# A fused two-layer transformer kernel: the delta rule of half the tokens moved between the second half's input products, the rest beside sparse attention and output products

## What is computed

```python
h = rmsnorm(x, g_pre) * (1.0 + scale) + shift
qkv_a, z_a, b_a, a_a, q_b, ckv, z_b, iq, ik, iw = split(h @ w_in)
# gated delta rule, 4 heads of 128, on silu(causal_conv(qkv_a, conv_w))
q, k = l2norm(q) * 128**-0.5, l2norm(k)
lmat = strict_lower((beta * k) @ k.T * decay)
tmat = inverse(eye + lmat)            # per chunk
v_new = tmat @ (beta * v) - (tmat @ (beta * k * exp(gc))) @ S
o = (q * exp(gc)) @ S + (q @ k.T * decay) @ v_new
S = S * exp(gc_last) + kg.T @ v_new
o_a = rmsnorm(o, g_gdn) * silu(z_a)
# sparse attention: per query the top keys by an index score, softmax with a
# distance bias over the compressed keys ckv, then w_uv
o_b = (softmax(q_b @ ckv.T * 128**-0.5 + bias, selected) @ ckv @ w_uv) * silu(z_b)
x = x + gate * rmsnorm(concat(o_a, o_b) @ w_out, g_post)
```

## Time and profile before

| what | us |
|---|---|
| median of three runs | 2534.99 |
| span of the profiled execution | 2543.5 |
| PE busy in it | 2028.3 (80%) |
| DVE busy | 1644.6 (65%) |
| ACT busy | 801.4 (32%) |
| POOL busy | 662.6 (26%) |
| `second_half` | from 2035.1 to about 2211.6 |
| `sparse` | to about 2263.9 |
| `delta` | to the end |

### The profile page before, as it was taken

One profiled execution on the slowest core, in us unless ns is written; L12 is line 12 of the kernel. 1 busy time (PEld: TensorE's weight loads), 2 busy tenths in 40 slices (PEclk: granted clock), 3 DMA queues, 4 the chain that ended last, 5 costly groups with the idle time before them and its releaser, 6 DMA issues. The chain is left out here.

```text
span 2543.5 us, 31869 instructions
## 1 busy us (share of the span) xinstructions
PE 2028.3 (80%) x11958; PEld 1321.8 (52%) x11958; DVE 1644.6 (65%) x3770; ACT 801.4 (32%) x1791; POOL 662.6 (26%) x657
## 2 busy tenths in 40 slices
PE   4999968696876798788698778859787688756886
PEld 3888858562331365454365456415333266636664
DVE  5668876589786766554768667587964417944442
ACT  2112220233423424532434543353222231231221
POOL 2222100233444333433333243343344200000000
PEclk9999989898987899999799888878999869977889
DMA  8998752399999999999899798999999833110000
GB/s 333 368 358 304 268 197 67 148 419 408 381 421 421 416 418 410 420 396 386 346 394 360 277 367 344 378 404 368 419 420 419 331 102 100 66 74 1 9 9 17
DMA packets 124682, 746.74 MB, mean 294 GB/s; under 512 B 13536, under 2 KB 16480, under 8 KB 56304
## 3 DMA queue, kind: packets, MB, share of 16 engines
q0 software_dynamic: 93792, 610.66, 60.2%
q1 hardware_dynamic: 30736, 134.05, 13.7%
HBM read 741.25 MB, written 3.41 MB: 293 GB/s over the span
## 5 line engine op out<-in xcount | busy, mean ns | idle before, releaser
L1766 POOL DMA_INDIRECT got<-in_peer_uv,idx x512 | 587.4, 1147 | 950.8 <-PE ps L1736 804.5
L1736 PE MATMUL ps<-got,diag 64*64 64x512 f32 x3936 | 607.8, 705 | 284.5 <-ACT diag L1823 266.3
L1860 DVE CUSTOM_DVE_ANT_0 got<-got,xk 128x1024 f32<-128x1024 f32 x512 | 616.1, 1221 | 253.5 <-DMA got<-in_peer_uv,idx 247.0
L1736 PEld LDWEIGHTS ps<-got,diag 64*64 64x64 f32 x3936 | 119.3, 146 | 564.0 <-ACT diag L1823 471.1
L1818 ACT ACTIVATE gelu<-eye,hid 128x64 f32<-128x64 f32 x492 | 169.9, 345 | 664.4 <-DVE hid L1860 662.9
L1325 PE MATMUL ps<-xT,ring 128*128 128x256 f32 x928 | 224.5, 393 | 6.6 <-DVE qkv L1414 6.6
L1325 PEld LDWEIGHTS ps<-xT,ring 128*128 128x128 f32 x928 | 173.7, 194 | 86.4 <-issue 48.0
L1027 PE MATMUL ps<-xT,ring 128*128 128x256 f32 x768 | 188.9, 395 | 1.7 <-ACT xT L1140 1.7
L1823 ACT ACTIVATE diag<-gelu,gate 128x64 f32<-128x64 f32 x492 | 171.1, 348 | 51.4 <-PE ps L1736 6.1
L1027 PEld LDWEIGHTS ps<-xT,ring 128*128 128x128 f32 x768 | 143.3, 194 | 77.1 <-issue 47.0
L192 POOL DMA_DIRECT2D vring<-in_vslabs x136 | 72.4, 533 | 275.3 <-DVE in_b_psums L304 139.5
(11 more groups left out here) (564 smaller groups left out, 2599.8 us busy)
## 6 DMA issues: line engine op xcount, KB each, us to landing
ring<-in_small SPq DMA_DIRECT2D x158, 512.0 KB, 7.9
vring<-in_vslabs POOLq DMA_DIRECT2D x136, 512.0 KB, 6.2
ring<-in_slabs SPq DMA_DIRECT2D x18, 2048.0 KB, 10.5
got<-in_peer_uv,idx POOLq DMA_INDIRECT x512, 13.2
h<-in_x SPq DMA_DIRECT2D x2, 2048.0 KB, 11.3
w_out<-in_slabs SPq DMA_DIRECT2D x2, 2048.0 KB, 11.3
out<-h SPq DMA_DIRECT2D x4, 512.0 KB, 2.6
bias_rows<-brow POOLq DMA_DIRECT2D x1, 1280.0 KB, 5.7
```

The costliest lines, as they stand in the source:

```text
L1736: mm = nc.tensor.matmul(ps[to:to + HALF, i, :], diag[own, d % NDIAG, :], got[own, n % GRING, 1, 512 * g:512 * g + 512], start=(k == 0), st ...
L1766: nc.gpsimd.indirect_dma_start(out=got[:, n % GRING].rearrange("p a d -> p (a d)"), out_offset=None, in_=table, in_offset=bass.IndirectOff ...
L1860: nc.vector.tensor_tensor_reduce(row_in, row_in, xk[:, w % 2, :], 1.0, 0.0, ALU.mult, ALU.add, hid[:, w % 2, k:k + 1]).then_inc(dotted, 1)
```

## The change

The delta rule is cut into functions of one step (`delta_tiles`), as are sparse attention (`sparse_tiles`), the output products (`mixed_tiles`) and the decay gates (`decay_gates`), and two blocks take the place of three stages.

- `second_half` carries, besides what it had, the decay gates of half a (steps 1 to 6) and of half b (45 to 49), the delta rule of tile 0 (steps 6 to 33) and tile 1 (33 to 60), one delta step per step, and sparse attention of tile 0 (48 to 62). PSUM: the delta rule has banks 0 to 2; the input products have 3 to 5 in turn (a product waits for the third before it); the rest shares 6 and 7.
- For half b the convolution's two copies and first tap are ScalarE's, with two buffers; VectorE keeps three taps. A product's bank is free once ScalarE has copied it.
- The Silu of half a's qkv and z_a move to the end of ScalarE's program in `peers`; half a's z_b and half b's qkv have theirs at step 57. Table sets are loaded by hand behind each.
- `gp_spread` and its product move from ahead of the steps to steps 20 to 23, the bias rows to every second step from 14.
- `recycle` is called between the two blocks.
- `second_rest` loads the output weights and walks one hand-made list of 43 steps: tiles 2 and 3 of the delta rule (tile 3 three steps behind), sparse attention of tiles 1 to 3, and output products of tiles 0 to 3. The output rows are squared by ScalarE out of PSUM and multiplied by the gain by VectorE out of PSUM, without a copy.
- In the head, row sums come ahead of the transposes, v is transposed at NORM, and the three token transposes wait each for their own operand.

```diff
@@ second_side
+        bank_of = lambda n: ps[:, 3 + (n - 4) % 3 if p and n >= 4 else 4 + n % 4, :]
+        back = 3 if p else 4
...
+                        elif p and second_jobs[before][0] == "qkv":
+                            pe.wait_ge(raw_out, second_jobs[before][1] + 1)
...
+                    elif p and kind == "qkv":
+                        mine = raw[:, i % 2, :]
+                        if i >= 2:
+                            act.wait_ge(dve_out, len(on_dve) + i - 1)
+                        step(nc.scalar.activation(mine[:, 0:3], halo[:, i, :], ACT.Copy))
+                        act.wait_ge(job_done, n - 3)
+                        nc.scalar.activation(mine[:, 3:3 + 2 * P], bank[:, 0:2 * P], ACT.Copy).then_inc(raw_out, 1)
+                        act.wait_ge(raw_out, i + 1)
+                        nc.scalar.activation(tap[:, i % 2, :], mine[:, 0:2 * P], ACT.Copy, scale=cw[:, 0, i:i + 1]).then_inc(tap_out, 1)
...
+                        mine, one = raw[:, i % 2, :], tap[:, i % 2, :]
+                        dve.wait_ge(tap_out, i + 1)
+                        for j in (1, 2):
+                            step(ve.scalar_tensor_tensor(one, mine[:, j:j + 2 * P], cw[:, j, i:i + 1], one, ALU.mult, ALU.add))
@@ peers, ScalarE
                     move(NW - 1)
+                    act.wait_ge(sides[2]["dve_out"], len(dve_jobs))
+                    for name in ("qkv", "z_a"):
+                        nc.scalar.activation(half_a[name], half_a[name], ACT.Silu)
@@ second_block
-                second_half(halves, whole, gp_row, gain_b, ckvT, score, bias, bias_loaded, w_uv, uv_loaded)
-                sparse(halves, whole["ckv"], ckvT, score, bias, bias_loaded, w_uv, uv_loaded)
-            delta(halves, whole["ba"], gain_b, gp_row)
+            second_half(halves, whole, gp_row, gain_b, ckvT, score, bias, w_uv, levels, state[:], gates)
+            recycle()
+            second_rest(halves, whole, gp_row, ckvT, score, bias, w_uv, levels, state[:], gates)
@@ delta_tiles
+            elif k == TURNS:
+                for b, x in enumerate(("qn", "kn", "xt")):
+                    pe.wait_ge(sg["tok"], 3 * u + b + 1)
+                    turn(b, tl[x]).then_inc(sg["nT"], 1)
...
+            elif k in LEVEL:
+                n = LEVEL[k][1]
+                pe.wait_ge(sg["yc"], (L - 1) * u + n)
...
+                if n < L - 1:
+                    heads(2, tl["xt"], tl["yc"]).then_inc(sg["za"], 1)
+                heads(0, tl["yc"], tl["xt"]).then_inc(sg["zb"], 1)
@@ mixed_tiles, VectorE
+            if k == MGAIN:
+                for part in range(2):
+                    dve.wait_ge(sq, 2 * t + part + 1)
+                    ve.tensor_tensor(here(t, part), by_head(ps[:, bank_of[t] + part, :]),
+                                     by_head(gp_row[:, 512 * part:512 * part + 512]), ALU.mult).then_inc(gained, 1)
@@ second_half
+            pre_at = {1: (0, PRE_A), 3: (0, PRE_B), 4: (0, PRE_C), 5: (0, PRE_D), 6: (0, PRE_E),
+                      45: (1, PRE_A), 46: (1, PRE_B), 47: (1, PRE_C), 48: (1, PRE_D), 49: (1, PRE_E)}
+            for s, k in ((6, GB), (6, RAW), (8, SQUARE), (9, EXPS), (10, NORM), (11, TOKEN), (12, TURNS), (13, LA), (14, EYE)):
+                delta_at.setdefault(s, []).append((0, k))
+            for k in range(EYE + 1, DSTEPS):
+                delta_at.setdefault(14 + k - EYE, []).append((0, k))
+            for k in range(DSTEPS):
+                delta_at.setdefault(14 + DLAST - EYE + k, []).append((1, k))
+            sparse_at = {s: k for s, k in ((48, FILL), (50, LOGIT0), (52, LOGIT1), (54, EXP), (56, SHARE), (58, TURN0), (60, VSUM),
+                                           (62, VALUE))}
...
-                        if s == GATE_A:
-                            for name in ("z_a", "z_b", "qkv"):
-                                nc.scalar.activation(half_a[name], half_a[name], ACT.Silu)
...
                         if s == GATE_QKV:
                             act.wait_ge(side["dve_out"], len(dve_jobs))
                             nc.scalar.activation(half_b["qkv"], half_b["qkv"], ACT.Silu)
+                            nc.scalar.activation(half_a["z_b"], half_a["z_b"], ACT.Silu)
+                            nc.scalar.preload_act_table_set("natural_log_exp_and_others")
@@ second_rest
+            delta = delta_tiles(st, "y", [[2], [3]], sets, halves, gates, levels, levels_seen, state, (egc_seen, 1))
+            sparse = sparse_tiles(st, "y", [1, 2, 3], 6, pr, prT, oT[:], halves, whole["ckv"], ckvT, score, bias, w_uv, freed, None)
+            mixed = mixed_tiles(st, {0: 6, 1: 6, 2: 0, 3: 3}, gp_row, w_out, w_out_loaded, inputs)
+            GAP = 3
+            when = [(k, 0, "delta", 2, k) for k in range(DSTEPS)] + [(k + GAP, 1, "delta", 3, k) for k in range(DSTEPS)]
+            of_sparse = {1: ((FILL, 0), (LOGIT0, 0), (LOGIT1, 1), (EXP, 2), (SHARE, 3), (TURN0, 4), (VSUM, 5), (VALUE, 6)),
+                         2: ((FILL, 6), (LOGIT0, 13), (LOGIT1, 14), (EXP, 15), (SHARE, 16), (TURN0, 17), (TURN1, 18), (VSUM, 19),
+                             (VALUE, 20)),
+                         3: ((FILL, 20), (LOGIT0, 27), (LOGIT1, 28), (EXP, 29), (SHARE, 30), (TURN0, 31), (TURN1, 32), (VSUM, 33),
+                             (VALUE, 34))}
+            for t, s in ((0, 7), (1, 21), (2, 29), (3, 35)):
+                when += [(s + k, 3, "mixed", t, k) for k in range(MEND + 1)]
+            when.sort()
```

1059 lines of the change are left out of this document (581 added, 478 removed).

## The result

The kernel after takes 2421.84 us (median of four, 2413.20 to 2423.08) where the kernel before takes 2535.22 beside it: 0.9533 of it, 95% interval 0.9503 to 0.9563. That is 113 to 118 us less, where I forecast 81 less and a range that ends at 2418; 0.9533 x 2534.99 is 2416.6, and the interval, 2409 to 2424, lies on both sides of that end. The profiled execution has a span of 2420.9 us, so here trace and median agree within 1 us, while that of before stood 8.5 above its median.

The account below looks back on a forecast made before the run. Round trips between TensorE and VectorE at a low clock bound the sparse and delta stages. Terms 2035.1 + 2.5 + 247 + 1.7 + 176 = 2462.3 against a 2543.5 us span, 81 us less, so 2454; range 2418 to 2500.

Parts of the forecast that it names:

- the first stage's head: Steps 0 to 12 of the first stage, with tile 0's gates and head added: 23.5 us where 19 stood.
- the boundary: Extra semaphore clearing with its barrier before the second stage: 1.7 us, bounds nothing or twice that.
- the Silu in the peers: Half a's table load and Silu at the end of the peer stage: +2.5 us.
- The stall per delta step: TensorE's wait at each of 86 delta steps in both stages: about 0.5 us a step, named as the unknown.
- steps 13 to 29: First stage, tile 0's matmuls between input products: 47 us plus 20 of matmuls and 4 of stalls, 71 us.
- the second stage's steps 12 to 20 and 21 to 26: Delta levels, sparse tile 2, state products, an output product: 41 us over 31 of TensorE, then 34 over 28.
- Steps 46 to 60: First stage, TensorE 44 us and VectorE 45 us in lock step, 13 us added for that: 58 us.
- 30 to 45: 48 us now: First stage, 48 us plus 11.5 of matmuls of tiles 0 and 1 and 7 of stalls: 66.5 us.
- The low clock at the heads: 9 us: Second stage, 9 us added for TensorE's low clock at the heads of its delta tiles.
- steps 0 to 11: Second stage's start: both heads, sparse tile 1 and the first output product, 43 us with stalls.
- rival B: Both stages: the clock holds at 2.4 GHz, 35 us more gain, 2419 us; chance 0.15.
- The switch of tables: Table loads priced at 1.28 us; the skill's 2.66 us at five switches would add 6.9 us, making 2461.

Follow-up runs that it names:

- e1: Kernel after with each level's ScalarE copy (y step) made twice, 24 copies more; 0.9555 of the kernel before, median 2427.0 us.
- e9: Kernel after with one more VectorE copy ahead of each level's subtraction into xn, 20 in all; 0.9564 of the kernel before, median 2428.2 us.
- e17: Kernel after with the split undone: VectorE subtracts only behind both products, the next y product waits for both; 0.9563 of the kernel before, median 2427.6 us.
- e16: Kernel before with only the split added: the product for xn signals by itself and the next y product waits for xn only; 0.9918, median 2517.3 us.
- e2: Kernel before with each level's ScalarE copy (y step) made twice, 24 copies more; 1.0109 of the kernel before, median 2564.4 us.
- e3: Kernel before with 148 useless identity matmuls put into the hops of the delta stage; 1.0008 of the kernel before, median 2539.2 us.
- e8: Kernel before with 64 useless identity matmuls, two instructions each, in the delta stage's hops; 0.9963 of the kernel before, median 2528.1 us.
- e14: Kernel after with useless identity matmuls where TensorE stands idle in the heads of both stages; 0.9534 of the kernel before, median 2424.7 us.

## Why the prediction was wrong, step by step

The sign, the order of size and the places were right: the first stage's head within 0.8 us, the boundary, the Silu in the peers, the products' waits for the convolution gone, VectorE as the limit of the last steps. The size was not. In the traces the forecast end was 2462.3 and it came at 2420.9: 41.4 us, of which 18.6 in the first stage, 21.4 in the second and 1.4 ahead of both. 9.4 us of that went again on the way from the trace to the median, which leaves the 32 us between 2454 and 2421.8. The sum itself is added up rightly.

**The stall per delta step.** This is the step that failed: "My stalls come to about 0.5 us a step", 43 us in 86 steps, taken near ScalarE's hop. In the view of TensorE's waits all that belong to the delta rule from 2081 on come to 11.3 us, 4.4 of them in one head, with 3.6 more ahead of 2081. By stretches: steps 13 to 29 had 4 us of stalls in the forecast and TensorE is idle for nothing of 65.1; the second stage's steps 12 to 20 and 21 to 26 had 10 and 6 us on top of TensorE's 31 and 28 and took 32.4 and 28.5, with 0.8 and 0.7 idle. The reason I gave for a small number was right ("most hops have other work of TensorE behind them") and I did not follow it to its end: a half of an input product is 1.74 us and both hops are shorter, so the stall is nothing, not a part of the hop. e1, e9 and e17 lengthen the hops by 14, 9 and up to 29 us in all and cost 2, 3.4 and 1.4 us behind the heads.

**Steps 46 to 60, "I add 13 us" for lock step.** 4.7 us are idle there (45.11 of 49.80). Nearly equal work on two engines cost a third of what I added.

**Stretches carried over at the old clock.** "13 to 29: 47 us now" was 47 us at 0.78 and "30 to 45: 48 us now" held 4.3 us of idle time; I added the new matmuls and stalls on top. In the trace after, the first of the two is TensorE full for 65.10 of 65.10 us at 0.88. Where products are added to a stretch that is not at the full clock, its old length is no constant: part of it goes when the clock comes.

**"The low clock at the heads: 9 us" in the second stage.** The clock is 0.96 over the stage and 0.85 in its first 21.7 us, about 3 us by that (an estimate, 21.7 x 0.15), and it is already in the 43.8 us of steps 0 to 11. The full clock from the first level on is rival B's; it gave 2419 at a chance of 0.15. Its number is close to the 2421.8 partly by luck: B took away only half of the stalls, where nearly all are gone, its "35 us" is more than its terms give (9 and half of 43, 30.5), and the first stage's head still runs at 0.65. Its direction is what happened, and it should have been the forecast: the earlier trace rows had the case in it, 1.00 and 0.98 in two stretches with TensorE busy 91% and 78%.

**The split of a level's signals** was not priced at all. It is worth next to nothing in the kernel after (e17) and 21 us in the kernel before (e16), and it is likely why the kernel with both overlaps undone is at 0.9923.

**The carry-over from trace to median.** I carried the 8.5 us over unchanged, but after the change the trace stands within 1 us of the median. The excess of before was in that one execution, in its tail, which is 5 to 10 us longer than the tails of e2, e3, e8 and e16 imply; a difference between one execution and its median is chance, not a property of the kernel.

**The switch of tables.** The load in the peers takes 1.28 us and the Silu starts 1.30 us behind its start (2029.75, 2031.05), the block ends 2.5 us later than VectorE's last. The Trainium skill, "ScalarE: Activation LUTs", section "What ACT_TABLE_LOAD costs", has about 2.66 us for a switch; this trace shows no drain here either.

What stays open: why the clock falls in the first stage's head with TensorE full, and whether anything but chance decides how long.

## What to carry to other kernels

A hop between engines cost next to nothing here once an independent piece of TensorE work longer than the hop stood behind it in the queue (1.74 us over hops of up to 1.5); price it at zero then, and check that by lengthening the hop rather than by arguing. It is not free where the engine that makes the hop is itself full. An open hop cost more than its length here, and TensorE's clock fell with it: in a chain without cover, let the next product wait only for the operand it needs, with a signal of its own, before moving whole stages about. And compare stages from a mark inside the trace, when what runs ahead of them scatters by more than the edit is worth; look for the mark behind which unchanged kernels repeat, here to 0.1 us where whole tails repeat to 3.

## What the hardware did that I had not expected

Useless matmuls made a kernel faster: 64 of them, 128 instructions in the hops of the kernel before, raised the clock of that stretch from 0.81 to 0.93 and took 9 us off the time, while 148 gave nothing. And behind its head the first stage, 183 us with 934 matmul instructions, repeats to 0.1 us from execution to execution, while the head ahead of it differs by 5. And in the head of the first stage the clock was at 0.52 for 12 us with TensorE busy all 12.00 us, behind 13 us at 1.00 with 9.49 busy (e14). The Trainium skill, "TensorE: Matmul & The Clock Gate", section "HAM oscillation — how this bites in real kernels", ties the low rate to idle gaps that recur; the trace of e2 agrees in that (0.77 with gaps of 1.32 and 1.47 us in its levels), this stretch does not show it.
